# A two-block transformer kernel without the unused identity products in TensorE's waits

## The reference

```python
# first block, each layer l, for latent and context tokens
hl = modulate(rms_norm(x_lat, norm1_g[l]), sh1, sc1)
pa, q, k, v, pc = project(hl, P, rope)                  # h @ w_in
o = blocked_diff_attn(q, k_all, v_all, lam)
x_lat = x_lat + g1 * mixer_merge(pa, o, pc, P, lam_init)
h2 = modulate(rms_norm(x_lat, norm2_g[l]), sh2, sc2)
x_lat = x_lat + g2 * conv_ffn(h2, P)
# second block, each layer i
h = x * (1.0 + sc1) + sh1
y, yc = _even_mixer(...) if i % 2 == 0 else _odd_mixer(...)
x = _layer_norm(DEEPNORM_ALPHA * x + g1 * y, p['ln1_g'], p['ln1_b'])
h = x * (1.0 + sc2) + sh2
x = _layer_norm(DEEPNORM_ALPHA * x + g2 * _conv_ffn(h, ...), p['ln2_g'], p['ln2_b'])
```

## Time and profile before

| | |
|---|---|
| median of 3 runs | 3516.88 us (3513.91 to 3517.04) |
| time of the profiled execution | 3513.67 us |
| its span, first to last instruction | 3511.8 us |
| TensorE busy | 3347.6 us, 95% of the span |
| VectorE, ScalarE, GpSimd busy | 2041.3, 1311.6, 432.6 us |
| TensorE's mean granted clock | 0.992 of full speed |

### The profile page before, as it was taken

The page is one execution under the profiler, slowest core; times in us unless marked ns, Lnnn a source line. Parts: engine busy times, 40 slices in busy tenths (PEclk is TensorE's granted clock), DMA queues, the critical chain, the costliest instruction groups (busy, mean ns, idle before and its releaser), DMA issues.

```text
span 3511.8 us, 47116 instructions
## 1 busy us (share of the span) xinstructions
PE 3347.6 (95%) x18692; PEld 2722.9 (78%) x18692; DVE 2041.3 (58%) x3251; ACT 1311.6 (37%) x2000; POOL 432.6 (12%) x387
## 2 busy tenths in 40 slices
PE   7998999999999999999998889999999999999998
PEld 5775888888887677888886577888888866668886
DVE  4757467545568647878435746654556455565345
ACT  3436342112234544223334544321223545444233
POOL 2005530000000320000003521000001023200000
PEclk9999999999999999999999999999999999999999
DMA  6440233333322113546221212442432311123332
GB/s 213 130 127 13 59 76 124 126 98 131 118 67 67 31 49 120 191 161 204 69 59 25 43 32 62 131 134 88 132 124 57 68 29 31 33 70 103 95 101 74
DMA packets 477242, 321.86 MB, mean 92 GB/s; under 512 B 54872, under 2 KB 450558, under 8 KB 477024
## 3 DMA queue, kind: packets, MB, share of 16 engines
q1 hardware_dynamic: 467104, 304.13, 28.6%
q0 software_dynamic: 9920, 14.71, 1.7%
HBM read 313.20 MB, written 3.57 MB: 90 GB/s over the span
## 4 chain that ended last, share of the span: by engine, by line
PE 81%; DVE 9%; ACT 5%; issue 3%; DMA 1%; POOL 1%; DVEq 0%; SPq 0%; ACTq 0%; POOLq 0%
PE PS L1161 78%; PE PS L1552 3%; DVE CPROD L3053 2%; DVE TMP L2743 1%; ACT BIG L2143 1%; DVE TMP L3371 1%; ACT TMP L2064 1%; DVE HL L2751 1%; DVE ATT L2875 1%; ACT SPH L1881 1%; ACT HH L2067 0%; DVE CACC L3151 0%; DMA XSTG<-in_x 0%; DMA RAW<-in_w_in 0%; DVE SPL L2558 0%
## 5 line engine op out<-in xcount | busy, mean ns | idle before, releaser
L1161 PE MATMUL PS<-HH,SPH 128*128 128x512 f32 (+1 forms) x3336 | 1138.3, 354 | 29.7 <-ACT HH L2067 11.3
L1161 PE MATMUL PS<-HL,SPH 128*128 128x512 f32 (+1 forms) x3336 | 1112.3, 352 | 3.8 <-DVE HL L2751 1.3
L1161 PEld LDWEIGHTS PS<-HH,SPH 128*128 128x128 f32 x3336 | 632.3, 190 | 142.2 <-issue 33.2
L1161 PE MATMUL PS<-HH,SPL 128*128 128x512 f32 (+1 forms) x3336 | 705.9, 354 | 0.0
L1161 PEld LDWEIGHTS PS<-HL,SPH 128*128 128x128 f32 x3336 | 628.6, 190 | 93.1 <-DVE HL L2751 8.5
L2558 DVE TENSOR_TENSOR SPL<-RAW,SPH 128x1024 fp32r<-128x1024 f32 (+3 forms) x358 | 447.1, 1249 | 333.3 <-ACT SPH L1881 333.2
L1161 PEld LDWEIGHTS PS<-HH,SPL 128*128 128x128 f32 x3336 | 560.9, 190 | 93.7 <-issue 7.6
L1881 ACT ACTIVATE SPH<-RAW 128x1024 fp32r<-128x1024 f32 (+3 forms) x358 | 383.7, 1072 | 522.3 <-PE PS L1161 449.5
L1161 PE MATMUL PS<-MH,SPH 128*128 128x512 f32 (+1 forms) x1067 | 362.5, 354 | 0.8 <-ACT SPH L1881 0.8
L1161 PE MATMUL PS<-ML,SPH 128*128 128x512 f32 (+1 forms) x1067 | 359.8, 352 | 0.0
L3371 DVE SCALAR_TENSOR_TENSOR TMP<-PS,PCOL,TMP 128x511 f32<-128x511 f32 (+1 forms) x264 | 174.3, 660 | 222.8 <-ACT TMP L2493 210.1
(11 more groups left out here) (360 smaller groups left out, 3639.9 us busy)
## 6 DMA issues: line engine op xcount, KB each, us to landing
MS<-in_mod_turned SPq DMA_DIRECT2D x144, 512.0 KB, 5.3
RAW<-in_l_w_up SPq DMA_DIRECT2D x88, 512.0 KB, 4.0
RAW<-in_w_gate SPq DMA_DIRECT2D x44, 512.0 KB, 4.2
RAW<-in_w_val SPq DMA_DIRECT2D x44, 512.0 KB, 4.2
RAW<-in_w_down SPq DMA_DIRECT2D x32, 704.0 KB, 4.7
RAW<-in_l_w_down SPq DMA_DIRECT2D x32, 704.0 KB, 4.6
RAW<-in_w_in SPq DMA_DIRECT2D x40, 512.0 KB, 4.6
MS<-in_w_mod SPq DMA_DIRECT2D x32, 512.0 KB, 4.7
```

The source lines that it names most:

```text
L1161: return pe.matmul(o, a, b, start=start, stop=stop)
```

## The change

`keep_clock` and all its calls go, with the argument `pause` of `linear` that carried one of them. No wait, no other instruction and no buffer changes; what stood behind the products now stands directly behind what was ahead of them.

```diff
-            def keep_clock(n, bank):
-
-                for _ in range(n):
-                    mm(bank[:, 0:P], IDENT, IDENT, True, True)
-
...
-            def linear(x, hi, lo, also=None, ready=None, order=range(DC), mid=None, chunk=None, spare=False, between=None, pause=0, before=None, ctx_ready=None):
+            def linear(x, hi, lo, also=None, ready=None, order=range(DC), mid=None, chunk=None, spare=False, between=None, before=None, ctx_ready=None):
                 def body(j, t, s):
-                    if j == 2:
-                        keep_clock(pause, AUX)
...
             def rms_sums(T):
 
                 rs_read()
-                keep_clock(10, LIN[0])
...
                 w.seen(S.inverse_ready)
-                keep_clock(15 if T == TOK else 11, LIN[0])
...
             def layer_norm_sums(x, T):
...
                 w.seen(S.inverse_ready)
-                keep_clock(15 if T == TOK else 10, AUX)
...
             def attention(A, L):
...
                 rs_read()
-                if A.mla:
-                    keep_clock(8, STAT)
...
-                    if n < 3:
-                        keep_clock(((13, 0, 0) if A.mla else (0, 0, 7) if A.diff else (0, 8, 0))[n], STAT if A.mla else AUX)
...
                     pe.wait_ge(S.row0_ready, 3)
-                    keep_clock(5, LIN[1])
                 elif l == 0:
                     turn_tokens(LAT // P, CTX // P, 2)
-                    keep_clock(12, LIN[0])
...
                         if n < 4:
                             head_sums(m0 + n, (4 + n,))
-                        if n == 4:
-                            keep_clock(8, AUX)
...
-                    linear(L["w_in"], HH, HL, None, S.h_ready, mid=latent_jobs, pause=9)
+                    linear(L["w_in"], HH, HL, None, S.h_ready, mid=latent_jobs)
...
                     query_spread(n0 + 1)
-                    keep_clock(14, AUX)
```

## The result

Without the products the kernel takes 3523.55 us (median of 16 runs, 3518.14 to 3527.04) against 3516.09 us for the kernel before in the same 16 rounds. Two executions of the kernel before stood far off, at 3782 and 7565 us, and the ratio leaves them out: it is 1.0022 (95% interval 1.0015 to 1.0029), or 7.7 us. The time is inside the predicted range (3514 to 3532) and 2.5 us above the predicted one. The change itself, forecast at +4.05 us, came out nearly twice as large, a little beyond the 0.2% that the prediction took as the border of no change.

A forecast was written before the change was run, and what follows sets the result against it. TensorE, busy for 95% of the span, was taken to set the time outside the attention stretches. Costs of clock falls, 6.5 us, less savings of 2.45 us gave +4.05 us on a base of 3516.88 us: 3521 us, range 3514 to 3532.

The forecast's parts named there:

- The three savings: Products holding work back at second block's start, third tile of last `w_in`, latent attention: 0.6, 1.2, 0.65 us, sum 2.45.
- The second block's start: Twelve products there hold back the lead by 0.6 us; without them a wait over 3 us brings a 1.6 us fall.
- the base: Median of the unchanged kernel's runs, 3516.88 us, to which the net change was added; the profiled execution took 3513.67 us.
- the norm at 3116 us: Ten products' length more of waiting: a certain fall in a lead fed chunk by chunk, counted half, 0.8 us.
- So a short wait costs a fall with a chance of 0.4.: Three waits, first layer's start and two `w_out` leads: 3 x 0.4 x 1.60 = 1.9 us; four of ten waits fell.
- A fall in attention of this kind costs 0.: First three layers' attention: VectorE, GpSimd and ScalarE pace it, so falls cost 0 (bound 1.6 us).
- The query projections: Fourteen products ahead of them: a certain fall, but TensorE catches up between chunks; between 0 and 1.6, taken as 0.8 us.
- each behind waiting: Claim that every stretch in the trace with TensorE's clock at 0.50 follows a wait; one fall priced at 1.60 us.
- only the long waits fall: Rival: short waits beside dense leads might never bring a fall, so the 1.9 us go; 3519 us, chance 0.10.
- The clock doesn't care: Rival: falls merely move in time, their number stays, only the savings count; 3514.4 us, chance 0.05.
- Faster than can be doubted: Rival: products delay more than seen, through bank or bus; a hidden third, 11 us, less half the costs; 3509 us, chance 0.06.
- every newly opened wait falls: Rival: all such waits on TensorE's path fall, some for double length; +14 us, 3531 us, chance 0.27.

The follow-up runs named there:

- The four groups: Kernel before less products at: three short waits, ratio 1.0004; first three layers' attention, 0.9999; three long waits, 1.0013; four layer norms, 1.0002.
- the first four experiments: Kernel before, each without one group of products: short waits 1.0004, first three layers' attention 0.9999, long waits 1.0013, layer norms 1.0002.
- the nine profiled executions: One each of the kernel before (3516.09 us), the changed kernel (3523.55 us) and the seven experiments' kernels (ratios 0.9979 to 1.0013).

## Why the prediction was right, and where it was not

The mechanism held but for one step, the attention: the products that held work back gave it back, the releasers of the other waits stayed, and at every removed place where the account rose, TensorE's clock had fallen. The three savings were predicted as 0.6, 1.2 and 0.65 us and showed as 0.63, 1.13 (in the changed kernel) and 0.75. The second block's start, 1.6 - 0.6, came out as 1.0. The sizes were worse than the time lets one think. The costs were put at 6.5 us; with 7.7 us net and 2.4 us saved they were about 10. The time came out nearer than that partly by luck, as the base was taken 0.8 us too high and the norm at 3116 us was overpriced. The four groups were also taken out one by one. Their runs give +1.5, -0.4, +4.6 and +0.7 us, and the two savings outside these groups about -1.8, which adds up to +4.6; with some 3 us of doubt on each of the four that neither contradicts 7.7 nor confirms it. The terms that were mis-sized:

- "So a short wait costs a fall with a chance of 0.4." In front of dense work it was five of six, 1.5 to 1.6 us each, 4.7 us in the changed kernel's trace instead of 1.9. Six of the ten waits behind the 0.4 were in attention, where two fell; of the other four two fell. They were not all of one kind.
- "A fall in attention of this kind costs 0." This step failed. The earlier trace rows compared two neighbouring pairs of steps, 9.38 and 9.39 us, one with the fall and one without, and took them to be alike. After the change the clock stays at 1.00 there (1190 to 1200 us above), and the maxima read:

```profile
1195.14 1.81 DVE L2856 TENSOR_REDUCE ATT<-PS 128x1 f32<-128x768 f32 x2
1198.92 1.81 DVE L2856 TENSOR_REDUCE ATT<-PS 128x1 f32<-128x768 f32 x2
1202.70 1.81 DVE L2856 TENSOR_REDUCE ATT<-PS 128x1 f32<-128x768 f32 x2
...
1212.07 1.82 DVE L2856 TENSOR_REDUCE ATT<-PS 128x1 f32<-128x768 f32 x2 [1.46 <-PE PS L1161]
```

  The pair that took 9.38 us with the fall takes 7.56 us without, and the next one 9.37. The early steps of this attention are faster than the later ones, and the fall had eaten just that. It cost the kernel before 2.05 us. At 1877 us a fall that the removal did open cost 2.25 us, where the sum has 0.
- The query projections were put at half a fall and cost 0.8 and 1.8 us; the norm at 3116 us was put at the same half and cost nothing. Both leads are fed chunk by chunk. How far TensorE catches up was guessed, not read.
- The base. The prediction took the rest of the kernel as unchanged. But falls elsewhere come and go by themselves: the pair at 359 and 372 us, worth 6.4 us, in two of the first four experiments and in neither the kernel before nor the changed one; one at 1264, worth 2.8; one at 2746, worth 1.6. Together with the landing of weights (1.6 us at 2785) they are large enough for the 3509 to 3522 us over which single runs of the kernel before range.
- "each behind waiting". The fall at 2746 us, which gave the price of 1.60 us, has no wait ahead of it. TensorE was busy for all of 2743 to 2746 us at full clock, with products of a single column:

```profile
2743.00:2746.00 3.00, 3.00 (x27) 2.88 (x26) 0.07 (x1) 0.00 (x0) 0.00 (x0) 1.00 0.54 154
...
2743.51 2.83 PE L1161 MATMUL PS<-CST,TMP 128*128 128x1 f32 x24
```

  In seven of the nine profiled executions the clock fell during these 24 products or within about 1 us of their end.

Of the rivals, "only the long waits fall" is out: short ones fell. "The clock doesn't care" is out. "Faster than can be doubted" is out: there was nothing hidden to gain. The one that every newly opened wait falls was nearly right on how often (not in the second layer's attention), and its 1.6 us were right where TensorE sets the time. The kernel stayed below its 3531 us because the norms and the first steps of attention cost little, and because a fall of the kernel before, at 1193 us, happened not to come.

The Trainium skill, "TensorE: Matmul & The Clock Gate", section "Terms", prices the time spent at the lower clock at half its length. The changed kernel spent 57 us more there, which by that rule would be 28 us, as an estimate; all runs say 7.7 us. The trace agrees for a stretch in which TensorE alone sets the time (1.5 to 1.6 us for 3.4 us of it). It doesn't for the leads behind the norms and the turns at the end: 23 of the 57 us lie there and cost 0.1 us.

Open: why the same wait brings a fall in one execution and none in the next, and why some falls last two or three times as long. No run here was made to settle it.

## What to carry to other kernels

An unused product in a wait is worth what follows it: dense TensorE work with nothing to catch up on (about 1.6 us for each wait here), not a lead that is paced by other engines (0 for fifty products). Count them so that they end when the data arrive. Where they outlast the wait they cost in full (2.5 us here), and three products fewer saved 0.6 us without a fall. Look for falls in the kernel as it is, too: covering three waits that it had left open gained 3.5 us (0.4 to 6.7), against 7.7 us for all the covers that it had. The costliest fall seen here, 4.7 us, stood among sums of a single column behind a wait of 1.44 us. To price a change of this size, subtract the starts of the same instructions of an unchanged engine in two traces, and do so for several executions.

## What was not expected

- At the head sums, products of a single column, the clock stood at half for ten us in two of seven executions, 2 us behind a wait of 1.44 us, and 4.7 us were lost, three times the price of a usual fall. The same wait brought nothing in the other five; why isn't shown.
- TensorE can fall to half clock while it is busy without a gap, behind 24 products of a single column.
- TensorE can stand at half clock for 10 us behind a norm instead of 3.4 and lose 0.0 us.
- A fall in attention cost 0, 0.66, 1.05, 2.05 and 2.25 us, depending on the step that it met and on its length.
- With 19 us less work on the engine that is busy for 95% of the span the kernel is 7.7 us slower.
